# Expert outputs scattered to token rows by indirect DMA, empty lanes skipped, and the last sums read back by plain loads

## What is computed

```
u2 = modulate(rmsnorm(x, norm_ffn_g), sh_ffn, sc_ffn)
e_idx, gw = route(u2)            # 32 experts in 8 groups: best group, top 2 experts inside it
h = silu(u2[tok] @ w_gate[e]) * (u2[tok] @ w_up[e])
x = x + gt_ffn * sum over the 2 experts of gw * (h @ w_down[e])
out = rmsnorm(x, final_g)
```

## Time and profile before

| | us |
|---|---|
| median of the 3 runs | 1627.49 |
| the 3 runs | 1622.82, 1627.49, 1628.82 |
| the profiled execution, its own time | 1622.71 |
| span in the profile, first to last instruction | 1620.9 |

### The profile page before, as it was taken

The page is one execution under the profiler, slowest core; times in us unless marked ns, Lnnn a source line. Parts: engine busy times, 40 slices in busy tenths (PEclk is TensorE's granted clock), DMA queues, the critical chain, the costliest instruction groups (busy, mean ns, idle before and its releaser), DMA issues.

```text
span 1620.9 us, 32501 instructions
## 1 busy us (share of the span) xinstructions
PE 1486.0 (92%) x12727; PEld 1052.6 (65%) x12727; DVE 815.1 (50%) x1192; ACT 437.4 (27%) x812; POOL 534.7 (33%) x458
## 2 busy tenths in 40 slices
PE   4899999999999999999998998499699798989994
PEld 3677787777778887787886886355355454545551
DVE  4655544555673324445223744455365544645556
ACT  5455553344461112002002321111111111111113
POOL 2532224333344323323231110244243333424453
PEclk9899999999999999999999998699899999989998
DMA  9570113222214333342121612999999999999997
GB/s 340 150 241 29 31 31 96 69 76 66 62 34 143 115 111 91 118 161 75 49 91 38 213 78 108 405 405 403 408 403 404 403 407 405 403 406 359 402 405 283
DMA packets 167551, 345.05 MB, mean 213 GB/s; under 512 B 28073, under 2 KB 96353, under 8 KB 159281
## 3 DMA queue, kind: packets, MB, share of 16 engines
q1 hardware_dynamic: 138544, 288.72, 47.7%
q0 software_dynamic: 19680, 37.65, 6.7%
q10 hardware_dynamic: 9248, 17.58, 3.5%
HBM read 311.41 MB, written 32.39 MB: 212 GB/s over the span
## 4 chain that ended last, share of the span: by engine, by line
PE 77%; DMA 11%; DVE 7%; ACT 2%; issue 2%; SPq 1%; POOL 1%; ACTq 0%; DVEq 0%; POOLq 0%
PE ps L822 30%; PE ps L1094 15%; DMA w_exp<-in_w_exp_up 8%; PE ps L991 7%; PE ps L1104 7%; PE ps L1015 4%; PE ps L886 2%; PE ps L859 2%; PE ps L1077 2%; PE ps L912 1%; PE ps L950 1%; PE ps L961 1%; PE ps L1084 1%; PE ps L873 1%; DVE br_lo L1608 1%
## 5 line engine op out<-in xcount | busy, mean ns | idle before, releaser
L1094 PE MATMUL ps<-w_exp,xT 128*32 128x256 f32 x4992 | 295.3, 390 | 40.5 <-DMA w_exp<-in_w_exp_up 34.6
L822 PE MATMUL ps<-u_hi,w_hi 128*128 128x512 f32 x768 | 308.5, 402 | 6.8 <-DVE u_lo L1513 6.6
L822 PE MATMUL ps<-u_hi,w_lo 128*128 128x512 f32 x768 | 300.3, 391 | 0.0
L822 PE MATMUL ps<-u_lo,w_hi 128*128 128x512 f32 x768 | 300.0, 391 | 0.0
L1094 PEld LDWEIGHTS ps<-w_exp,xT 128*32 128x32 f32 x4992 | 158.0, 112 | 146.4 <-issue 51.3
L614 POOL CAST w_hi<-w_raw 128x1024 fp32r<-128x1024 f32 x48 | 62.5, 1301 | 382.9 <-PE ps L822 232.7
L1852 DVE COPY w_down<-w_exp 128x4096 f32<-128x4096 f32 x78 | 179.7, 2304 | 0.0
L822 PEld LDWEIGHTS ps<-u_hi,w_hi 128*128 128x128 f32 x768 | 144.9, 189 | 45.3 <-issue 9.7
L822 PEld LDWEIGHTS ps<-u_hi,w_lo 128*128 128x128 f32 x768 | 144.7, 188 | 31.1
L822 PEld LDWEIGHTS ps<-u_lo,w_hi 128*128 128x128 f32 x768 | 145.1, 189 | 29.3 <-issue 1.0
L1104 PE MATMUL ps<-w_down,actT 128*32 128x256 f32 x2496 | 150.9, 382 | 2.7 <-DVE w_down L1852 2.7
(11 more groups left out here) (282 smaller groups left out, 2131.3 us busy)
## 6 DMA issues: line engine op xcount, KB each, us to landing
w_exp<-in_w_exp_gate SPq DMA_DIRECT2D x32, 2048.0 KB, 26.6
w_exp<-in_w_exp_up SPq DMA_DIRECT2D x32, 2048.0 KB, 29.3
w_exp<-in_w_exp_down SPq DMA_DIRECT2D x32, 2048.0 KB, 28.7
ada_g<-in_ada_w ACTq DMA_DIRECT2D x32, 512.0 KB, 3.7
w_raw<-in_w_in SPq DMA_DIRECT2D x24, 512.0 KB, 4.1
w_raw<-in_w_branch_gate SPq DMA_DIRECT2D x24, 512.0 KB, 4.0
d_y<-yb POOLq DMA_DIRECT2D x78, 128.0 KB, 8.6
bias<-d_table SPq DMA_DIRECT2D x48, 192.0 KB
```

Source lines behind the costliest of these rows:

```text
L822: ins = pe.matmul(ps[:, 5 + h, :], a[par][:, kc, :], b[:, kc, HF[h]], start=(n == 1), stop=(n == MM))
L1094: last = pe.matmul(ps[CAP * n:CAP * (n + 1), 2, 0:QT], x, w[n // 2][:, off:off + QT], start=(kc == 0), stop=(kc == KC - 1))
```

## The change

`d_y` gets one row for each token and rank of expert, 2 x 1024 rows. The store of a block is an indirect DMA that writes each quarter row to the place of its token. Its row numbers are a second table, and both tables lie in `rows_of`. An empty lane gets a number past the end in both (`AWAY` = 16384 is added to all, and taken off where there is a token); `bounds_check` with `oob_is_err=False` makes gather and store leave such rows out. The zeros at the start are no longer written. The last reads of `d_y` are plain loads issued by SP, and POOL issues no gathers at the end. ScalarE and SP now count in `rounds`, the number of couples of blocks less two, since `st_y` starts from zero.

```
-SPARE = 4 * P
+AWAY = 16384
...
-        tokl = at("tokl", 203.25, [P, LIST], i32)
-        count_i = at("count_i", 191.25, [P, LIST], i32)
-        count_f = at("count_f", 203.875, [P, LIST])
+        rows_of = at("rows_of", 203.25, [P, 2, LIST], i32)
+        count_i = at("count_i", 203.25, [P, LIST], i32)
+        count_f = at("count_f", 191.25, [P, LIST])
...
-        d_y = nc.dram_tensor("d_y", (NBLK * CAP, D), f32, kind="Internal").ap()
+        d_y = nc.dram_tensor("d_y", (2 * T, D), f32, kind="Internal").ap()
...
+        y_rows = d_y.rearrange("t (q n) -> (t q) n", q=4)
+        y_d = d_y.rearrange("(k t p) d -> k p t d", k=2, p=P)
...
-            for h in range(2):
-                sp.wait_ge(st_y[h], 32)
...
+            rounds = sp.value_load(starts[0:1, NE + 2:NE + 3], min_val=NE // 2 - 1, max_val=NBLK // 2 - 2)
+            early_free = sp.value_load(starts[0:1, NE - 2:NE - 1], min_val=NE, max_val=NBLK + 1)
+            sp.wait_ge(gu_ps, early_free)
+            hold(sp)
+            for h in range(2):
+                sp.wait_ge(st_y[h], rounds * 16)
+                hold(sp)
+            for t in range(TT):
+                sp.dma_start(y1[t][:], y_d[1, :, t, :]).then_inc(ld_early, 16)
+            for h in range(2):
+                sp.wait_ge(st_y[h], rounds * 16 + 32)
+                hold(sp)
+            for t in range(TT):
+                sp.dma_start(y0[t][:], y_d[0, :, t, :]).then_inc(ld_late[t], 16)
...
-            pool.wait_ge(zero_set, 1)
-            for h in range(2):
-                for part in range(2):
-
-                    first = (NE + 2) * CAP + SPARE * (2 * h + part)
-                    rows = d_y[first:first + SPARE, :].rearrange("(p k) (a n) -> p (k a) n", p=P, n=2 * P)
-                    pool.dma_start(rows, zero_row[:].unsqueeze(1).to_broadcast([P, SPARE * D // P // (2 * P), 2 * P])).then_inc(st_y[h], 16)
...
-            early_free = pool.value_load(starts[0:1, NE - 2:NE - 1], min_val=NE, max_val=NBLK + 1)
...
-                pool.tensor_copy(tok_cur[:, h:h + 1], tokl[:, col]).then_inc(tok_ready, 1)
+                pool.tensor_copy(tok_cur[:, h:h + 1], rows_of[:, 0, col]).then_inc(tok_ready, 1)
                 pool.wait_ge(tok_ready, n)
                 hold(pool)
                 pool.indirect_dma_start(out=xg[h][:], out_offset=None, in_=u2_rows,
-                                        in_offset=bass.IndirectOffsetOnAxis(ap=tok_cur[:, h:h + 1], axis=0)).then_inc(ld_xg[h], 16)
-
-            def store_outputs(h, row, n):
-
-                pool.wait_ge(yb_ready, n)
+                                        in_offset=bass.IndirectOffsetOnAxis(ap=tok_cur[:, h:h + 1], axis=0),
+                                        bounds_check=4 * T - 1, oob_is_err=False).then_inc(ld_xg[h], 16)
+
+            def store_outputs(h, col, evac, n):
+
+                pool.wait_ge(yb_ready, evac)
                 hold(pool)
-                pool.dma_start(d_y[row, :].rearrange("t (n m) -> n t m", n=4), yb[h][:]).then_inc(st_y[h], 16)
+                pool.tensor_copy(row_cur[:, h:h + 1], rows_of[:, 1, col]).then_inc(tok_ready, 1)
+                pool.wait_ge(tok_ready, n)
+                hold(pool)
+                pool.indirect_dma_start(out=y_rows, out_offset=bass.IndirectOffsetOnAxis(ap=row_cur[:, h:h + 1], axis=0),
+                                        in_=yb[h][:], in_offset=None,
+                                        bounds_check=8 * T - 1, oob_is_err=False).then_inc(st_y[h], 16)
 
             for b in range(2):
                 gather_rows(b, slice(b, b + 1), None, b + 1)
@@ -742,32 +752,13 @@
             for b in range(4, 6):
                 gather_rows(b % 2, slice(b, b + 1), b, b + 1)
                 if b == 5:
-                    store_outputs(0, slice(0, CAP), 5)
+                    store_outputs(0, slice(0, 1), 5, 7)
             with pool.Fori(3, n_couples + 1) as q:
                 for h in range(2):
-                    gather_rows(h, bass.ds(q * 2 + h, 1), q * 2 + h, q * 2 + (h + 1))
-                    store_outputs(1 - h, bass.ds(q * (2 * CAP) + (h - 5) * CAP, CAP), q * 2 + h)
-            def last_rows(b):
-
-                store_outputs((b + 1) % 2, bass.ds(n_couples * (2 * CAP) + (b - 3) * CAP, CAP), n_couples * 2 + (b + 2))
-
-            pool.wait_ge(gu_ps, early_free)
-            hold(pool)
-            for h in range(2):
-                pool.wait_ge(st_y[h], n_couples * 16)
-                hold(pool)
-            for t in range(TT):
-                pool.indirect_dma_start(out=y1[t][:], out_offset=None, in_=d_y,
-                                        in_offset=bass.IndirectOffsetOnAxis(ap=pair_s[:, 1, t:t + 1], axis=0)).then_inc(ld_early, 16)
-                if t % 4 == 3:
-                    last_rows(t // 4)
-            last_rows(2)
-            for h in range(2):
-                pool.wait_ge(st_y[h], n_couples * 16 + 32)
-                hold(pool)
-            for t in range(TT):
-                pool.indirect_dma_start(out=y0[t][:], out_offset=None, in_=d_y,
-                                        in_offset=bass.IndirectOffsetOnAxis(ap=pair_s[:, 0, t:t + 1], axis=0)).then_inc(ld_late[t], 16)
+                    gather_rows(h, bass.ds(q * 2 + h, 1), q * 2 + h, q * 4 + (2 * h - 4))
+                    store_outputs(1 - h, bass.ds(q * 2 + (h - 5), 1), q * 2 + h, q * 4 + (2 * h - 3))
+            for b in range(3):
+                store_outputs((b + 1) % 2, bass.ds(n_couples * 2 + (b - 3), 1), n_couples * 2 + (b + 2), n_couples * 4 + b)
...
-            sc.wait_ge(starts_ready, 1)
-            n_couples = sc.value_load(starts[0:1, NE + 1:NE + 2], min_val=NE // 2 + 1, max_val=NBLK // 2)
+            sc.wait_ge(slots_ready, 2)
+            rounds = sc.value_load(starts[0:1, NE + 2:NE + 3], min_val=NE // 2 - 1, max_val=NBLK // 2 - 2)
...
-                    output_rows((b - 1) % 2, b + 2, 48 if b == 3 else None)
-            with sc.Fori(3, n_couples + 1) as q:
+                    output_rows((b - 1) % 2, b + 2, 16 if b == 3 else None)
+            with sc.Fori(1, rounds + 1) as q:
                 for h in range(2):
-                    silu(q * 2 + h)
-                    next_rows(h, None, q * 16 + 16, q * 2 + h)
-                    output_rows(1 - h, q * 2 + h, q * 16 + 16 * h)
-            output_rows(1, n_couples * 2 + 2, n_couples * 16 + 16)
+                    silu(q * 2 + (h + 4))
+                    next_rows(h, None, q * 16 + 48, q * 2 + (h + 4))
+                    output_rows(1 - h, q * 2 + (h + 4), q * 16 + 16 * h)
+            output_rows(1, rounds * 2 + 6, rounds * 16 + 16)
...
+            ch(dve.tensor_scalar(quarter_f[:], quarter_f[:], float(AWAY), None, ADD))
...
-            ch(dve.tensor_copy(tok4[:], tok[:]))
-            ch(dve.tensor_scalar(tok4[:], tok4[:], 4.0, None, MUL))
+            ch(dve.tensor_scalar(quarter_f[:], quarter_f[:], float(AWAY), None, ADD))
+            ch(dve.tensor_copy(tok4[:, 0, :], tok[:]))
+            ch.mark(dve.tensor_scalar(tok4[:, 1, :], tok4[:, 0, :], 4.0, float(4 * T - AWAY), MUL, ADD))
+            ch(dve.tensor_scalar(tok4[:, 0, :], tok4[:, 0, :], 4.0, float(-AWAY), MUL, ADD))
...
-                ch.mark(dve.tensor_tensor(own, own, tok4[:].unsqueeze(2).to_broadcast([P, TT, CAP]), MUL))
+                ch.mark(dve.tensor_tensor(own, own, tok4[:, k, :].unsqueeze(2).to_broadcast([P, TT, CAP]), MUL))
...
-            dve.tensor_scalar(tokl[:], ps[:, 2, 0:LIST], quarter_f[:], None, ADD).then_inc(tok_ready4, 1)
+            ch(dve.tensor_scalar(rows_of[:, 1, :], ps[:, 2, 0:LIST], quarter_f[:], None, ADD))
+            dve.tensor_single_scalar(rows_of[:, 0, :], rows_of[:, 1, :], AWAY + 4 * T - 1, ALU.bitwise_and).then_inc(tok_ready4, 1)
...
-            dve.sem_inc(slots_ready, 1)
+            dve.tensor_scalar(starts[:, NE + 2:NE + 3], starts[:, NE + 1:NE + 2], 2.0, None, SUB).then_inc(slots_ready, 1)
```

More of the change, by code:

```diff
@@ L170, in build @@
         t_a, t_b, t_c, t_d = (at(f"t_{n}", 64 + 4 * i, [P, T]) for i, n in enumerate("abcd"))
-        zero_row = at("zero_row", 203, [P, 2 * P])
         merged = at("merged", 128, [P, KC, T])
@@ L246, in build @@
         turn = at("turn", 190.875, [P, 2 * TT])
-        tok4 = at("tok4", 191, [P, TT])
+        tok4 = at("tok4", 191, [P, 2, TT])
         first_rank = at("first_rank", 191.125, [P, EPG])
@@ L290, in build @@
         tok_cur = small("tok_cur", [P, 2], i32)
+        row_cur = small("row_cur", [P, 2], i32)
         tok = small("tok", [P, TT], i32)
@@ L295, in build @@
         pair_s = small("pair_s", [P, 2, TT], i32)
-        starts = small("starts", [1, NE + 2], i32)
+        starts = small("starts", [1, NE + 3], i32)
         ps = ctx.enter_context(nc.psum_tensor("ps", [P, 8, HALF], f32))
@@ L342, in build @@
             "ld_rt", "score_ready", "hit_ready", "rank_ps", "count_ready", "slots_ready", "half_hits", "list_ps", "starts_ready", "tok_ready"))
-        zero_set = sem("zero_set")
         ld_wt = [sem(f"e_ld{r}") for r in range(RING)]
```

(3 more changed lines are left out.)

## The result

The changed kernel takes 1612.58 us (median of 6 runs, 1606.96 to 1615.48), the kernel before 1625.55 beside it (6 runs, 1622.82 to 1630.33). The ratio is 0.9919, with a 95% interval of 0.9894 to 0.9943: about 13 us or 0.8% faster. The prediction was 1623.7 us, with 1614 to 1630 as its range. The profiled execution after took 1612.94 us, with a span of 1611.0.

A forecast was written before the change was run, and what follows sets the result against it. Bound by full DMA queues until 1437 us, then PE block after block until the end part. Terms -2.5 - 1.5 + 0.25 = -3.75 us, applied to the median 1627.49, gave 1623.7 us, range 1614 to 1630.

The forecast's parts named there:

- 405 GB/s as a fixed rate: Expert stage: DMA queues are full whether PE works or waits, so saved bytes were turned into time at 405 GB/s.
- Part 1, the empty lanes: Weight-bound stretch before 1437 us: leaving out empty lanes saves 2.6 MB; 2.5 us gained, bounds 0 and 6.4.
- the rival of all engines relieved: Left out rows free the last DMA engines too: part 1 gives 6.4 us, part 3 3.5; total 1617.8 us; chance 0.2.
- No relief at all: Rival: left out lanes give 0 in the weight-bound stretch and 1 us at the end; 1626.7 us; chance 0.25.
- Part 2, POOL's work: Per block, the indirect store adds 0.65 us to POOL, fitting by 0.8 us under PE's 6.26; cost 0.
- POOL would become the bound: Rival: indirect DMAs above about 1.4 us use up POOL's room per block; at 2.0 us, +50 us, 1677; chance 0.1.
- Part 3, the end: After the last blocks: earlier `y1`, last store and `y0` together gain 1.5 us; bounds 5 gained, 1 lost.
- the same by plain loads: End part: `y1`'s 4.2 MB take 10.4 us at 405 GB/s by plain loads too; sooner only by saved bytes, 1 us.
- The wait of the last `yb`: End part: without sixteen gathers in POOL's queue, the last `yb` need not wait 7.36 us for a held-up store.
- Part 4, routing: Before the first gather: a second VectorE operation for `rows_of` costs 0.25 us, bounds 0.2 and 0.4.
- Part 5, the zeros: Start of the kernel: 8 MB less written gives 0, covered by PE's projection matmuls.
- weight waits that shrink by more than 5 us: Sign of a wrong forecast: PE's weight-load idle time before line 1094 was expected to fall from 49 to about 46.

The follow-up runs named there:

- e1: Changed kernel, but every lane given a row, empty ones gathering some token row and storing to spare rows; expert part 524.6 us, median 9.6 us under the kernel before.
- e5: Kernel before, with only the plain store's destination walked in address order, not with a stride; expert part 524.3 us against 531.4, median gains 6.4 us.
- e7: Changed kernel, but POOL gathers `y1` and `y0` as before instead of SP's plain loads; ratio 0.9964 to the kernel before.
- e8: Changed kernel, with the 8 MB of zeros written again to a buffer nobody reads, with the old waits; 1611.81 us, ratio 0.9941.
- e4: Changed kernel, with tokens dealt to lanes 0, 4, 8 and so on, then 1, 5, 9, so empty lanes are spread; 1604.86 us, expert part 520.2.
- e10: The spread-lane kernel (0, 4, 8, then 1, 5, 9) run again beside the changed kernel on one chip; 1609.63 us, expert part 520.6.
- e12: Changed kernel, with tokens dealt to lanes 28, 24, 20 down to 0, then 29, 25, 21, so empty lanes are spread; 1608.6 us, expert part 519.7.

## Why the prediction was wrong

The forecast was a gain of 3.75 us. Measured it is 13 by the medians, or 9.1 + 4.0 + 0.6 = 13.7 us in the expert and end parts of the traces. Some 2 us of the distance between 1623.7 and 1612.58 is the kernel before itself, which took 1625.55 in these runs and not 1627.49. Point by point:

**The step that failed: the change part by part, in what it removes.** The sum costed the lanes and POOL's time of the old store, and had no term for the store's effect on the DMA engines. It took 405 GB/s as a fixed rate, because it was the same beside a busy and an idle PE. It was this kernel's rate: the strided form of the store kept it at 405, by its small packets, by the few large ones that it has in flight, or both. The indirect store (e1) and a plain one in address order (e5) both reach 412, and each takes 7 us off the expert part. The row that hinted at it was the earlier trace rows: 8.6 us for the landing of a 128 KB store, where a gather of as much took 6.1. I used 8.6 as a latency and did not ask why a write took 40% longer than a read of the same size. Neither end of the range had this term, and so the result lies below the range by 1.4 us.

**Part 1, the empty lanes: right.** 2.5 us taken, 2.3 measured against e1 (1.1 to 2.5 with e7 and e8), between the ends 0 and 6.4. The size agrees within the scatter of 1.4 us, which is too wide to prove it. One premise the trace does show: a left out row costs next to nothing. A packet of four left out rows takes 11 ns in the kernel after, a full one 167. The reason given for 2.5 and for the lower end of 0, that relief of some engines only helps where these were the last, is shown by no row and no run: none tells which DMA engine moves which lanes, or which was last. So the 2.5 was an estimate between 0 and 6.4. What the runs show in its place is 2.3 us with the empty lanes at the high end, and 1.5 to 2.6 us more than the change with spread ones (e4, e10 and e12), where left out rows shorten 308 of q0's packets in 100 us instead of 36. The full 6.4 us was not reached even then (4.0 to 4.9 from e1), so the rival of all engines relieved overstates it. No relief at all is not borne out either, since 2 us came.

**Part 2, POOL's work: right.** It cost nothing that shows: the period of a block stays at 6.27 us, and an indirect DMA takes 1.02 us with its check of 128 numbers, far from the 1.4 at which POOL would become the bound. The margin was as small as computed, but it sits elsewhere: it is the copy of the row numbers, not the store, that falls under VectorE's copy (1.7 us instead of 0.18), and 0.42 us of POOL's block is left as a wait.

**Part 3, the end: too small, for want of two terms.** 1.5 us taken, 4.0 + 0.6 measured, near the bound of 5. I held that `y1` comes sooner only by saved bytes and gave that 1 us. For the kernel before that holds: its engines are full up to the last bytes. But with 1.6% more rate the backlog is smaller: e5 alone, with POOL's gathers, gets from 19.3 to 16.3 us. This follows from the failed step. The other term is the plain loads, which I put at nothing ("the same by plain loads"): had POOL kept the gathers beside its new indirect stores, `y1` would have been added after 19.1 us (e7). So the plain loads are worth 3.8 us in the changed kernel, by keeping what the indirect stores would have cost. The wait of the last `yb` (7.36 us) vanished as said.

**Part 4, routing: right.** 0.25 us taken, 38.87 to 39.08 is 0.2 measured.

**Part 5, the zeros: not contradicted.** 0 taken; e8 shows no cost beyond its scatter.

The measured sum in the traces: 7 us for the store's form in the expert part, 2 for the lanes, 4 to 5 at the end, less 0.2 for routing. Among the signs of a wrong prediction stood "weight waits that shrink by more than 5 us", and that is what came (49.0 to 41.9).

## What to carry to other kernels

Where DMA is the bound, ask of each transfer in what packets it goes and how many of them are in flight at once, not only how many bytes it has. A small side stream can lower the rate of the large one: here the stores and gathers are 9% of the bytes, and the strided form of the stores took 1.6% off the whole rate. A rate that is constant over a kernel need not be the chip's limit, and a write that lands much later than a read of the same size is a reason to look at the packets by size and queue. When an indirect DMA takes the place of a plain one, count the issuing engine's time around both sides of the edit: it was free while POOL had 0.4 us left per block and would have cost 4 us where POOL also issued the last reads.

## What the runs showed of the hardware that was not expected

- A plain store of 128 KB with a destination of shape 4 x 32 x 256 whose outer stride is less than its middle one makes 96 packets of 16 B beside its 32 of 4 KB, has at most 4 of the large ones in flight at once (18 stores; e5: 7 to 14), and lands in 8.6 us instead of 6.2 in address order.
- Rows left out by the bounds check save bytes but no packets: q0 moved 3.19 MB in 1341 packets with them left out, and 3.54 MB in 1300 without (e1), and over the whole span both have 157951 packets, with 332.64 and 336.55 MB. The sizes fit packets of four rows of 1 KB (4096 B) in which each row left out leaves 4 bytes (3076 B with one left out): in 100 us of the kernel after there are 100 packets of 16 B (11 ns each) and 36 of 1036, 2056 or 3076 B, and with spread lanes (e4) none of 16 B and 308 of the others. So the small packets rose from 721 to 834, and not where lanes were spread (735).
- An indirect DMA with the check takes POOL some 0.03 to 0.05 us more: 1.02 us for a store and 1.04 for a gather in a block of the kernel after, 0.99 for a gather before. Only the gathers compare like with like.
- A copy of 128 int32 on POOL takes 0.18 us alone and 1.7 us when it meets VectorE's copy of 128x4096 float32.
